# Two transformer blocks in split fp32r: shifting where operands begin in on-chip memory, by multiples of 16 bytes

## The reference

```
def swiglu(x, wi, wo):
    gate, up = jnp.split(x @ wi, 2, axis=-1)        # 1024 -> 2 x 2816
    return (jax.nn.silu(gate) * up) @ wo            # 2816 -> 1024
...
for li in range(2):                                 # first block
    h = h + 0.5 * swiglu(rms_norm(h, ffn1_norm[li]), ...)   # units a1, b1
    h = h + mixer(rms_norm(h, mix_norm[li]))                # li 0: gated linear attention + pooling, li 1: sparse attention
    h = h + 0.5 * swiglu(rms_norm(h, ffn2_norm[li]), ...)   # units a2, b2
h = rms_norm(h, final_norm)
...
x = x + 0.5 * swiglu_2(rms_norm_2(x, ...), ...)             # second block: unit c1
x = x + (gated sum of two attentions) @ w_o
x = x + 0.5 * swiglu_2(rms_norm_2(x, ...), ...)             # unit c2
```

## Time and profile before

| | |
|---|---|
| two runs | 1460.72 and 1460.99 us |
| span of the profiled execution | 1458.9 us, first to last instruction |
| what a run's time holds beside the span | 2.0 us (1460.86 - 1458.9) |
| TensorE matmul / weight load busy | 1452.6 / 1250.3 us |
| VectorE / ScalarE / GpSimd busy | 1002.6 / 778.5 / 87.2 us |
| granted TensorE clock | 1.00 throughout |
| HBM read | 264.56 MB, 182 GB/s |

### The profile page before, as it was taken

How to read it: one execution, slowest core, us unless ns; L and a number is a source line. 1 busy time by engine, 2 the same in 40 slices (tenths; PEclk the granted TensorE clock), 3 DMA queues, 4 the chain that set the end, 5 groups by cost and what they waited for, 6 DMA issues and landing times.

```text
span 1458.9 us, 18627 instructions
## 1 busy us (share of the span) xinstructions
PE 1452.6 (100%) x7822; PEld 1250.3 (86%) x7822; DVE 1002.6 (69%) x1216; ACT 778.5 (53%) x971; POOL 87.2 (6%) x113
## 2 busy tenths in 40 slices
PE   9999999999999999999999999999999999999999
PEld 7888888888888888888888888888888888888887
DVE  6976466787755867459877664787646987687653
ACT  6654355655534555345665544564435876465542
POOL 0000003000000000006100000000000800000000
PEclk9999999999999999999999999999999999999999
DMA  9855563556556555545455556475556543556552
GB/s 328 277 183 178 160 203 116 168 180 201 179 182 202 187 187 189 186 139 172 150 198 188 189 172 206 154 223 182 187 173 217 188 144 118 173 193 205 178 187 72
DMA packets 205620, 266.82 MB, mean 183 GB/s; under 512 B 6944, under 2 KB 148880, under 8 KB 205280
## 3 DMA queue, kind: packets, MB, share of 16 engines
q1 hardware_dynamic: 204320, 261.23, 54.5%
q0 software_dynamic: 1072, 4.35, 0.8%
q10 hardware_dynamic: 144, 0.05, 0.0%
HBM read 264.56 MB, written 1.05 MB: 182 GB/s over the span
## 4 chain that ended last, share of the span: by engine, by line
PE 96%; DVE 2%; ACT 1%; DMA 0%; issue 0%; DVEq 0%; ACTq 0%
PE ps L637 33%; PE ps L643 17%; PE ps L563 14%; PE ps L565 13%; PE ps L564 13%; PE ps L616 1%; PE ps L717 1%; PE ps L812 1%; DVE wlo L1632 1%; PE ps L750 1%; DVE d_i L2025 0%; DVE d_m L2021 0%; DMA G<-in_gains 0%; DVE d_i L2049 0%; PE ps L751 0%
## 5 line engine op out<-in xcount | busy, mean ns | idle before, releaser
L1632 DVE TENSOR_TENSOR wlo<-raw,whi 128x2048 fp32r<-128x2048 f32 (+5 forms) x275 | 567.4, 2068 | 259.0 <-ACT whi L1193 258.6
L1193 ACT CAST whi<-raw 128x2048 fp32r<-128x2048 f32 (+5 forms) x275 | 474.7, 1732 | 222.8 <-PE ps L565 218.4
L637 PE MATMUL ps<-xt,whi 128*128 128x512 f32 x2112 | 511.2, 391 | 0.5 <-DVE xt L2225 0.5
L637 PEld LDWEIGHTS ps<-xt,whi 128*128 128x128 f32 x2112 | 386.0, 188 | 74.4 <-DVE xt L2225 1.3
L643 PEld LDWEIGHTS ps<-xt,wlo 128*128 128x128 f32 x2112 | 274.0, 191 | 12.3
L643 PE MATMUL ps<-xt,wlo 128*128 128x256 f32 x2112 | 277.7, 283 | 0.0
L563 PE MATMUL ps<-whi,xt 128*128 128x512 f32 (+4 forms) x304 | 112.7, 371 | 0.0
L565 PE MATMUL ps<-whi,xt 128*128 128x512 f32 (+4 forms) x304 | 109.7, 361 | 0.0
L564 PE MATMUL ps<-wlo,xt 128*128 128x512 f32 (+4 forms) x304 | 109.5, 360 | 0.0
L563 PEld LDWEIGHTS ps<-whi,xt 128*128 128x128 f32 x304 | 57.3, 188 | 9.2 <-issue 1.0
L565 PEld LDWEIGHTS ps<-whi,xt 128*128 128x128 f32 x304 | 57.2, 188 | 8.5
(11 more groups left out here) (422 smaller groups left out, 1885.8 us busy)
## 6 DMA issues: line engine op xcount, KB each, us to landing
raw<-in_ffn_wi SPq DMA_DIRECT2D x85, 1024.0 KB, 4.9
raw<-in_ffn_wo SPq DMA_DIRECT2D x40, 1024.0 KB, 5.0
raw<-in_ffn_w_gate SPq DMA_DIRECT2D x22, 1024.0 KB, 5.1
raw<-in_ffn_w_up SPq DMA_DIRECT2D x22, 1024.0 KB, 5.2
raw<-in_ffn_w_down SPq DMA_DIRECT2D x20, 1024.0 KB, 4.9
raw<-in_w_in SPq DMA_DIRECT2D x14, 1024.0 KB, 5.1
raw<-in_even_w_in SPq DMA_DIRECT2D x6, 1024.0 KB, 5.2
raw<-in_ffn_wo SPq DMA_DIRECT2D x8, 512.0 KB, 3.8
```

What stands on the lines that cost most here:

```text
L637: return e.matmul(pair.ap[:, b, :], whi[:, v % SPLIT, 256 * j + 128 * b:256 * j + 128 * b + 128], XS[:, j, :, :].rearrange("p h t -> p (h ...
L1193: e.copy(whi[0:n, v % SPLIT, c], raw[0:n, v % RAW, c]).then_inc(s_hi.mark(*[(v, j) for j in js]), 1)
L1632: e.tensor_tensor(wlo[0:n, v % SPLIT, c], raw[0:n, v % RAW, c], whi[0:n, v % SPLIT, c].bitcast(F32), ALU.subtract).then_inc(s_lo.mark(*[(v ...
```

## The change

No instruction is added or removed, and the order on every engine stays. Three sorts of tile begin elsewhere:

| unit | `xt` shifted by, bytes | `ht_hi`, `ht_lo` begin at, bytes mod 512 | `wlo` in gate and up | `wlo` in down |
|---|---|---|---|---|
| a1 | 0 | 96, 96 | 0 to 336 | 0, 48, 96, ... |
| a2 | 0 | 160, 160 | 352 to 688 (mod 512) | the same |
| b1 | 192 | 224, 224 | 0 to 336 | the same |
| b2 | 256 | 320, 320 | 352 to 688 (mod 512) | the same |
| c1 | 384 | 0, 256 | 0 to 336 | the same |
| c2 | 448 | 256, 0 | 352 to 688 (mod 512) | the same |

In gate and up each following slot's low part begins 16 bytes further, in down 48 bytes further, modulo 512. The mixers keep `xt`, `yt` and `wlo` at multiples of 512 bytes, and `whi` stays there everywhere. Other tiles of the mixers move with the layout, by 448 bytes modulo 512. `wlo`, `xt` and `ht` get room for the shifts; to pay for it `P1` of the last mixer now lies in half of the tile `m_fk`, and `kr_room` and `FT` in `P0`, so that ScalarE and not VectorE waits for `("kr", 1)`.

```diff
+PAD = 128
+X_AT = {"in": 0, "gla": 0, "a2": 48, "dsa": 64, "b2": 96, "mla": 112}
+H_AT = {"in": (24, 24), "gla": (40, 40), "a2": (56, 56), "dsa": (80, 80), "b2": (0, 64), "mla": (64, 0)}
...
     def room(self, sb):
-        self.hT = Turned(sb(self.name + "ht_hi", [128, 22, 256], F32R), sb(self.name + "ht_lo", [128, 22, 256], F32R))
+        def part(i, name):
+            at = (H_AT[self.x][i] - 112) % PAD
+            return sb(self.name + name, [128, 22 * 256 + PAD], F32R)[:, at:at + 22 * 256].rearrange("p (k t) -> p k t", k=22)
+
+        self.hT = Turned(part(0, "ht_hi"), part(1, "ht_lo"))
...
-        wlo = sb("wlo", [128, SPLIT, 2048], F32R)
+        wlo_room = sb("wlo", [128, SPLIT, 2048 + PAD], F32R)
...
-        XS = sb("xt", [128, 8, 2, 256], F32R)
-        XT = Turned(XS[:, :, 0, :], XS[:, :, 1, :])
...
+        xs_room = sb("xt", [128, 4096 + 112], F32R)
+
+        def x_turned(x):
+            at = X_AT.get(x, 0)
+            XS = xs_room[:, at:at + 4096].rearrange("p (k h t) -> p k h t", k=8, h=2)
...
+        def low_at(v):
+
+            job, i = plan[v]
+            f = next((f for f in (a1, a2, b1, b2, c1, c2) if job in f.g + f.u + f.d), None)
+            if f is None:
+                at = 0
+            elif job in f.d:
+                at = 12 * (6 * f.d.index(job) + i) % PAD
+            else:
+                at = 4 * (2 * int(job.name[3:]) + (job in f.u) + (22 if f in (a2, b2, c2) else 0)) % PAD
+            return wlo_room[:, v % SPLIT, at:at + 2048]
...
-                    hi_w, lo_w = (w[0:n, v % SPLIT, j * wd:(j + 1) * wd] for w in (whi, wlo))
+                    hi_w, lo_w = (w[0:n, j * wd:(j + 1) * wd] for w in (whi[:, v % SPLIT, :], low_at(v)))
...
-                        e.matmul(pair.ap[:, b, 0:256], wlo[:, v % SPLIT, 256 * j + 128 * b:256 * j + 128 * b + 128],
-                                 XS[:, j, 0, :], start=False, stop=False)
+                        e.matmul(pair.ap[:, b, 0:256], low_at(v)[:, 256 * j + 128 * b:256 * j + 128 * b + 128],
+                                 f.XS[:, j, 0, :], start=False, stop=False)
...
-            kr_room = [mat.P1[:, 0, 0:32], mat.P1[:, 0, 32:64]]
-            FT = mat.P1[:, 1:3, 0:80]
+            mat = Attention("m_", lambda n, s: sb(n, s, F32, sc), (FQ[:, :, :].rearrange("p b n -> p (b n)"), FK[:, 0, :]),
+                            FK[:, 1, :].rearrange("p (h t) -> p h t", h=4))
+            kr_room = [mat.P0[:, 0, 0:32], mat.P0[:, 0, 32:64]]
+            FT = mat.P0[:, 1:3, 0:80]
```

More of the change, by code:

```diff
@@ L156, in __init__ @@
     def __init__(self, name, x, gate, g0, up, u0, down, XT):
-        self.name, self.x = name, x
-        self.g = [Job(f"{name}g{i}", gate, [(0, 8, 128)], [(g0 + 256 * i, 256)], XT, ("xt", x)) for i in range(11)]
-        self.u = [Job(f"{name}u{i}", up, [(0, 8, 128)], [(u0 + 256 * i, 256)], XT, ("xt", x)) for i in range(11)]
+        self.name, self.x, self.XS = name, x, XT[x].XS
+        self.g = [Job(f"{name}g{i}", gate, [(0, 8, 128)], [(g0 + 256 * i, 256)], XT[x], ("xt", x)) for i in range(11)]
+        self.u = [Job(f"{name}u{i}", up, [(0, 8, 128)], [(u0 + 256 * i, 256)], XT[x], ("xt", x)) for i in range(11)]
         self.d = [Job(f"{name}d{i}", down, full_blocks(FF), [(512 * i, 512)], None, (name, "ht")) for i in range(2)]
@@ L243, in program @@
         whole = sb("whole", [128, 96])
+        xs_room = sb("xt", [128, 4096 + 112], F32R)
+        def x_turned(x):
+            at = X_AT.get(x, 0)
+            XS = xs_room[:, at:at + 4096].rearrange("p (k h t) -> p k h t", k=8, h=2)
+            t = Turned(XS[:, :, 0, :], XS[:, :, 1, :])
+            t.XS = XS
+            return t
+        XT = {x: x_turned(x) for x in ("in", "a1", "gla", "a2", "b1", "dsa", "b2", "c1", "mixed", "mla")}
         def col_jobs(name, w, K, ranges, act, key):
@@ L257, in program @@
         ga, gk, gu, gv, gg = col_jobs("gla", T["even_w_in"][0], D,
-                                      [[(1536, 16), (0, 256)], (256, 256), (1552, 512), (512, 512), (1024, 512)], XT, ("xt", "a1"))
+                                      [[(1536, 16), (0, 256)], (256, 256), (1552, 512), (512, 512), (1024, 512)], XT["a1"], ("xt", "a1"))
         g_out = col_jobs("gla_out", T["even_w_out"][0], D, [(0, 512), (512, 512)], YT, ("yt", "gla"))
@@ L262, in program @@
         di, dk, dq0, dq1, dv = col_jobs("dsa", T["odd_w_in"][0], D,
-                                        [(1536, 324), (1024, 256), (0, 512), (512, 512), (1280, 256)], XT, ("xt", "b1"))
+                                        [(1536, 324), (1024, 256), (0, 512), (512, 512), (1280, 256)], XT["b1"], ("xt", "b1"))
         d_out = col_jobs("dsa_out", T["odd_w_out"][0], D, [(0, 512), (512, 512)], YT, ("yt", "dsa"))
         lat, fq, fk, fv, *gate2 = col_jobs("mla", T["w_in_2"][0], D, [[(0, 352), (1888, 8)], (352, 512), (864, 512), (1376, 512)]
-                                           + [(1896 + 512 * i, 512) for i in range(4)], XT, ("xt", "c1"))
+                                           + [(1896 + 512 * i, 512) for i in range(4)], XT["c1"], ("xt", "c1"))
         qb = [Job(f"qb{i}", T["mla_w_qb_2"][0], [(0, 2, (128, 64))], [c], YT, ("yt", "lat")) for i, c in enumerate([(0, 512), (512, 256)])]
@@ L272, in program @@
             j.k_off = 4
-        c_out = col_jobs("c_out", T["w_o_2"][0], D, [(0, 512), (512, 512)], XT, ("xt", "mixed"))
+        c_out = col_jobs("c_out", T["w_o_2"][0], D, [(0, 512), (512, 512)], XT["mixed"], ("xt", "mixed"))
         def together(a, b):
@@ L346, in program, with __init__ @@
         class Attention:
-            def __init__(self, name, room, second=None):
+            def __init__(self, name, room, second=None, p1=None):
                 self.name = name
@@ L357, in __init__ @@
                 self.P0 = room(name + "P0", [128, 4, 256])
-                self.P1 = room(name + "P1", [128, 4, 128])
+                self.P1 = room(name + "P1", [128, 4, 128]) if p1 is None else p1
                 self.nm = room(name + "nm", [128, 16])
@@ L441, in program @@
             q_room = [LAT[:, 0, 0:256], LAT[:, 1, 0:256]]
-            mat = Attention("m_", lambda n, s: sb(n, s, F32, sc), (FQ[:, :, :].rearrange("p b n -> p (b n)"), FK[:, 0, :]))
-            kr_room = [mat.P1[:, 0, 0:32], mat.P1[:, 0, 32:64]]
-            FT = mat.P1[:, 1:3, 0:80]
+            mat = Attention("m_", lambda n, s: sb(n, s, F32, sc), (FQ[:, :, :].rearrange("p b n -> p (b n)"), FK[:, 0, :]),
+                            FK[:, 1, :].rearrange("p (h t) -> p h t", h=4))
+            kr_room = [mat.P0[:, 0, 0:32], mat.P0[:, 0, 32:64]]
+            FT = mat.P0[:, 1:3, 0:80]
         with ExitStack() as sc:
@@ L577, in last_steps @@
                         q.wait_ge(*s_lo[v, j])
-                        hi_w, lo_w = (w[:, v % SPLIT, j * wd + c0:j * wd + c0 + n] for w in (whi, wlo))
+                        hi_w, lo_w = (w[:, j * wd + c0:j * wd + c0 + n] for w in (whi[:, v % SPLIT, :], low_at(v)))
                         h, l = (a[:, kt, 128 * tt:128 * tt + 128] for a in (job.act.hi, job.act.lo))
@@ L597, in by_tiles @@
                         q.wait_ge(*s_lo[v, j])
-                        hi_w, lo_w = (w[:, v % SPLIT, j * wd:(j + 1) * wd] for w in (whi, wlo))
+                        hi_w, lo_w = (w[:, j * wd:(j + 1) * wd] for w in (whi[:, v % SPLIT, :], low_at(v)))
                         h, l = (a[:, kt, 128 * tt:128 * tt + 128] for a in (job.act.hi, job.act.lo))
@@ L637, in high @@
                         return e.matmul(pair.ap[:, b, :], whi[:, v % SPLIT, 256 * j + 128 * b:256 * j + 128 * b + 128],
-                                        XS[:, j, :, :].rearrange("p h t -> p (h t)"), start=j == 0, stop=j == 7)
+                                        f.XS[:, j, :, :].rearrange("p h t -> p (h t)"), start=j == 0, stop=j == 7)
                     def low(j, b):
@@ L1210, in turn_x @@
                 q.wait_ge(*s_dve["gains"])
-                turned(("xt", x, n), XT, 4 * n, lambda i: gains_of[x](4 * n + i))
+                turned(("xt", x, n), XT[x], 4 * n, lambda i: gains_of[x](4 * n + i))
             def squares(x, n):
@@ L1537, in mla @@
                 softmax(mat, ("f", 1), 1)
+                q.wait_ge(*s_pool["kr", 1])
                 probabilities(mat, ("f", 0))
@@ L1571, in mla @@
                 unit()
-                turned(("mixt", 0), XT, 0, None)
+                turned(("mixt", 0), XT["mixed"], 0, None)
                 unit()
                 unit()
-                turned(("mixt", 1), XT, 4, None)
+                turned(("mixt", 1), XT["mixed"], 4, None)
                 unit()
@@ L1589, in x_high @@
                 q.wait_ge(*s_xt[min(j // 2, 2)]["x"])
-                e.mul(XT.hi[:, j, :], XR[:, j, :], gain("f1", j)).then_inc(s_act.mark(("x0", j)), 1)
+                e.mul(XT["in"].hi[:, j, :], XR[:, j, :], gain("f1", j)).then_inc(s_act.mark(("x0", j)), 1)
             x_high(0)
@@ L1631, in low @@
                 q.wait_ge(*s_hi[v, js[0]])
```

(11 more changed lines are left out.)

## The result

The changed kernel takes 1471.2 us (1470.99 and 1471.40), the kernel before 1460.86: ratio 1.0071, 95% interval 1.0055 to 1.0087. It is **10.3 us slower**; 8.0 us were forecast (1468.9). The profiled execution spans 1469.2 us against 1458.9.

The account below looks back on a forecast made before the run. TensorE was taken to bound the kernel, through the distances between matmul starts. Terms 5.6 + 1.4 + 2.7 - 1.7 = +8.0 us gave span 1466.9 and, with 2.0 carried over, 1468.9 us (predicted 1469, range 1446 to 1480).

Parts of the forecast that it names:

- Term 1: Down in a1, a2, b1, b2: ht offset from whi puts 1056 matmuls out of rhythm, 5.3 ns each, +5.6 us.
- Term 2: Down in c1, c2: moving wlo puts one matmul in three out of rhythm; half price, 528 x 2.65 ns, +1.4 us.
- Term 3: Line 637 in b1 and c2: shifted xt against whi takes 704 matmuls from 228.1 to 232.0 ns, +2.7 us.
- Term 4: Line 643, 256 columns: swept wlo puts 2112 matmuls out of rhythm, 0.8 ns less each, -1.7 us.
- 5, 6, the rest: Casts and subtractions into shifted wlo, and ScalarE taking over the ("kr", 1) wait: both covered by slack, 0 us.
- the measure of 128 bytes: Feed-forward wide matmuls: offsets between operands that are multiples of 128 bytes were taken to cost nothing.
- addresses do not matter: 360-column difference in the mixers is only mixed widths settling; time 1460.9 us, within 2 us; no effect had chance 0.24.
- The equal addresses are what costs: Feed-forward reads collide at equal places; offsets gain -19 us, 1441.7; partial gain 0.20, gain over 2% 0.05.
- A slower rhythm: Offset wide matmuls settle 13.33 ns higher, 240.0 ns for 512 columns: +23.5 us, 1484, or 1500.8; chance 0.09.

Follow-up runs that it names:

- first survey: Changed kernel with xt at 16 to 96 bytes and ht at 16 to 112, one offset per unit, whi and wlo at 0: 1474.0 us.
- second survey: Changed kernel with xt 64 bytes off in all units, whi and ht at 0, wlo in gate and up swept by 16 bytes a slot: 1460.8 us.

## Why the prediction was right, and where it was not

The sum held, 8.0 us against 10.3, and its mechanism too: TensorE bounds everything, addresses act on the distance between matmuls, wide ones lose some 5 ns when their operands begin at different places, narrow ones gain a little. By its steps:

| term | forecast, us | changed kernel, us | how measured |
|---|---|---|---|
| 1, down in a1, a2, b1, b2 | +5.6 | +5.2 | 61.5 + 61.6 + 61.3 + 61.2 - 4 x 60.1 |
| 2, down in c1, c2 | +1.4 | +2.5 | c1 +1.3, c2 +1.2 |
| 3, line 637 | +2.7 | +4.8 | page, 516.0 - 511.2 |
| 4, line 643 | -1.7 | -2.6 | page, 275.1 - 277.7 |
| 5, 6, the rest | 0 | 0 | no-shift run, 1460.57 |
| sum | +8.0 | +9.9 | spans differ by 10.3 |

- **Term 1** was sized right, with luck: the starts of a1's down stand 232.4 ns apart on average, forecast 232.0. The 5.3 ns came from matmuls that had not settled and from another width. With one fixed offset down holds another steady distance, 233.3 ns (first survey), and `ht` alone costs +7.0 us in the whole kernel; with `wlo` swept beside it the price falls to what was forecast.
- **Term 2 was mis-sized**, by the assumption that a shifted operand in one matmul of three costs half. It costs the full +1.3 a unit, because the two matmuls beside it leave the rhythm too: in c1 the distances after lines 591, 592 and 593 average 231.0, 232.6 and 231.3 ns, all above 226.7. With `wlo` alone the six units pay it likewise (+6.1 us with the gain of line 671 taken off).
- **Term 3 was mis-sized**, by the measure of 128 bytes, which I had only from 13.33 ns being the time of 32 columns. The measure is 256 bytes: `xt` at 256 costs nothing, at 384 the full price, and the run with 128 bytes everywhere costs 15.8 us. c1 was left out of the sum for that reason; its runs of line 665 average 3.72 us instead of 3.65, some 1.5 us in 22 slots. The rest is size: b1's matmuls stand (573.59 - 569.86) / 16 = 233.1 ns apart, forecast 232.0.
- **Term 4**: the sign held. It is a mean over slots that differ by offset, from 1.82 us a run (c2, 1340.95 to 1342.77) to 1.92 (b2, 843.82 to 845.74), where equal places take 1.91.
- **Rows 6 did not show all that I took from them.** The contrast, 160.0 ns with equal and 165.3 with shifted addresses, was taken as address alone. In the changed kernel block 0 of the 360-column slot has equal addresses as before, but follows a down stage out of rhythm:
```profile
1111.43 0.33 PE L591 MATMUL ps<-whi,xt 128*128 128x360 f32 x1
...
1112.41 0.33 PE L591 MATMUL ps<-whi,xt 128*128 128x360 f32 x1
```
Its six matmuls take 0.98 us by these rows, 164.7 ns each in the unrounded trace. The run with everything moved by 192 bytes shows the same, though its down stage in c1 averages 226.8 ns; there the place changes between the two stages, from 192 to 0:
```profile
1103.35 0.32 PE L598 MATMUL ps<-whi,xt 128*128 128x360 f32 x1
...
1104.33 0.33 PE L598 MATMUL ps<-whi,xt 128*128 128x360 f32 x1
```
In the six other runs in which c1's down keeps to equal places (no shift, `ht` alone, `xt` alone, `whi` with `xt`, `wlo` at 208, the second survey) block 0 takes 160.0 to 160.3 ns, in the others 164 to 165. The price belongs to the rhythm being lost, by an address or by what went before.

The sum is near for these reasons together: terms 2 and 3 were 3.2 us too small, against which term 1 came 0.4 lower and term 4 gained 0.9 more than forecast.

Of the rivals, "addresses do not matter" fell when the run without shifts gave back all that the change cost. With it falls, for this kernel, the rule of two independent read ports (the Trainium skill, "TensorE: Matmul & The Clock Gate", Step-by-step: what each phase is for), if it is read as saying that the two reads cannot hinder each other: runs that differ in addresses alone lie between 1452.7 and 1476.6 us. "The equal addresses are what costs" is wrong for wide matmuls, of which none fell clearly below 226.7 ns at any offset tried, and right for narrow ones at some offsets only: 116.9 ns at 208 bytes and 113.8 at 192, but 120.0 at 96, where equal places give 119.4; the trace of before could not tell the two widths apart, since its narrow matmuls all had equal addresses. "A slower rhythm" was half right: 240.0 ns was nowhere a unit's mean, but 233.3, half that step above 226.7, was held by five units of the first survey.

## What to carry to other kernels

Where TensorE is full, read the distance between starts and subtract the columns at the clock; what is left can depend on where the two operands begin relative to each other. Compare stretches of the same shape with different offsets before choosing one, and set the offset for each width by itself: here only the low parts, read with 256 moving columns, gained by one. A sweep over many offsets averages gains and losses and looks like little; its value is the table that it leaves.

## What the runs showed of the hardware

- The offset counts modulo 256 bytes, as far as tried: with `xt` alone shifted, 0 and 256 took 3.65 us a run of line 665, 192 and 384 took 3.72 and 3.73; `ht` at 0 and 256 gave 60.1 us.
- The relation counts, not the place: all operands of the feed-forward units 192 bytes further, 1460.95 us.
- The distance depends on state too: the same addresses gave 113.8 ns a matmul after out-of-rhythm wide matmuls and 118.1 after settled ones, and 1.81 and 1.88 us in neighbouring slots.
- The steadiest distances were whole multiples of 6.67 ns: 226.7 (34), 120.0 (18), 160.0 (24) and, new, 233.3 (35) and about 113.3 (17). Others, such as the 118.1 with `whi` moved along, are none.
- In down other engines' writes are not the cause: 233.3 ns with VectorE, ScalarE and GpSimd idle (`ht` at 112 bytes). What inside TensorE or on the way to it makes the relation count, these runs do not say.
